# Unread products of thirteen widths in the gap behind the down projection

## The reference, cut to what matters

```python
def rmsnorm(x, g, eps=EPS):
    xf = x.astype(jnp.float32)
    y = xf * lax.rsqrt(jnp.mean(xf * xf, axis=-1, keepdims=True) + eps)
    return (y * g.astype(jnp.float32)).astype(x.dtype)

def conv_gated_ffn(h, w_gate, w_up, w_conv, w_down):
    g = causal_dwconv(h @ w_gate, w_conv)
    return (jax.nn.silu(g) * (h @ w_up)) @ w_down
...
    h = h + rmsnorm(f, g_post_ffn[layer])
...
    h = rmsnorm_2(x, norm_mix_g[l])
    proj = jnp.einsum('bsd,de->bse', h, w_in[l])
```

## Time and profile before

| what | us |
|---|---|
| median of 2 runs | 3160.98 (3160.81 to 3161.16) |
| the profiled execution: its own time | 3160.61 |
| its span, first to last instruction | 3158.8 |
| matmul engine busy | 3145.9 |
| VectorE busy | 2146.8 |
| ScalarE busy | 1823.7 |
| GpSimd busy | 457.4 |
| granted clock of the matmul engine, mean share of full speed | 0.999 |

### The profile page before, as it was taken

How to read it: one execution, slowest core, us unless ns; L and a number is a source line. 1 busy time by engine, 2 the same in 40 slices (tenths; PEclk the granted TensorE clock), 3 DMA queues, 4 the chain that set the end, 5 groups by cost and what they waited for, 6 DMA issues and landing times.

```text
span 3158.8 us, 58846 instructions
## 1 busy us (share of the span) xinstructions
PE 3145.9 (100%) x24156; PEld 3007.3 (95%) x24156; DVE 2146.8 (68%) x3503; ACT 1823.7 (58%) x2611; POOL 457.4 (14%) x317
## 2 busy tenths in 40 slices
PE   9999999999999999999999999999999999999998
PEld 9999999999999999999999999999999888888887
DVE  7987486666664477665666799855555666668886
ACT  6556554444444455555455578877777544456565
POOL 0001200000000100000000057777770000000000
PEclk9999999999999999999999999999999999999999
DMA  6444556666666656444555577787776777766554
GB/s 226 156 147 146 178 182 233 230 223 230 229 197 196 193 174 206 164 153 167 187 196 199 199 190 195 196 195 194 194 194 196 243 242 241 242 226 224 212 186 171
DMA packets 229420, 627.78 MB, mean 199 GB/s; under 512 B 59328, under 2 KB 78624, under 8 KB 229024
## 3 DMA queue, kind: packets, MB, share of 16 engines
q1 hardware_dynamic: 192144, 623.60, 59.1%
q0 software_dynamic: 36864, 0.15, 3.2%
q10 hardware_dynamic: 144, 0.26, 0.0%
HBM read 601.27 MB, written 21.10 MB: 197 GB/s over the span
## 4 chain that ended last, share of the span: by engine, by line
PE 98%; DVE 1%; ACT 1%; issue 0%; DMA 0%; POOL 0%; SPq 0%; DVEq 0%; ACTq 0%; POOLq 0%
PE ps L981 32%; PE ps L982 32%; PE ps L983 31%; DVE wl L1562 0%; PE ps L1265 0%; PE ps L1288 0%; PE ps L1285 0%; PE ps L1022 0%; PE ps L1052 0%; PE ps L1299 0%; PE ps L1289 0%; DMA raw<-in_in1k 0%; PE ps L1065 0%; PE ps L1461 0%; PE ps L1119 0%
## 5 line engine op out<-in xcount | busy, mean ns | idle before, releaser
L2402 ACT CAST wh<-raw 128x1024 fp32r<-128x1024 f32 (+3 forms) x1094 | 1137.4, 1040 | 1024.4 <-PE ps L983 1020.1
L1562 DVE TENSOR_TENSOR wl<-raw,wh 128x1024 fp32r<-128x1024 f32 (+2 forms) x863 | 1037.0, 1203 | 362.1 <-ACT wh L2402 359.5
L981 PE MATMUL ps<-xh,wh 128*128 128x256 f32 x3088 | 854.9, 277 | 0.5 <-issue 0.5
L983 PE MATMUL ps<-xh,wl 128*128 128x256 f32 x3088 | 850.0, 275 | 0.0
L982 PE MATMUL ps<-xl,wh 128*128 128x256 f32 x3088 | 849.9, 275 | 0.0
L981 PE MATMUL ps<-xw,wh 128*128 128x258 f32 (+2 forms) x2096 | 591.4, 282 | 1.8 <-issue 1.1
L983 PE MATMUL ps<-xw,wl 128*128 128x258 f32 (+2 forms) x2096 | 587.7, 280 | 0.0
L981 PEld LDWEIGHTS ps<-xh,wh 128*128 128x128 f32 x3088 | 579.7, 188 | 4.3 <-issue 1.6
L982 PEld LDWEIGHTS ps<-xl,wh 128*128 128x128 f32 x3088 | 579.8, 188 | 1.1 <-issue 1.0
L983 PEld LDWEIGHTS ps<-xh,wl 128*128 128x128 f32 x3088 | 579.6, 188 | 0.0
L2930 POOL DMA_INDIRECT table<-w_loose x256 | 397.8, 1554 | 805.3 <-DVE w_loose L2237 654.4
(11 more groups left out here) (425 smaller groups left out, 4678.0 us busy)
## 6 DMA issues: line engine op xcount, KB each, us to landing
raw<-in_peer_u SPq DMA_DIRECT2D x256, 512.0 KB, 4.7
raw<-in_peer_v SPq DMA_DIRECT2D x236, 512.0 KB, 4.2
raw<-in_w_in SPq DMA_DIRECT2D x172, 512.0 KB, 3.6
raw<-in_w_up SPq DMA_DIRECT2D x82, 512.0 KB, 4.8
raw<-in_w_gate SPq DMA_DIRECT2D x80, 512.0 KB, 4.5
raw<-in_w_down SPq DMA_DIRECT2D x80, 512.0 KB, 3.7
raw<-in_w_out SPq DMA_DIRECT2D x64, 512.0 KB, 3.7
table<-tmp SPq DMA_DIRECT2D x32, 512.0 KB, 6.3
```

Source lines behind the costliest of these rows:

```text
L981: t.matmul(o, lh, rh, start=start, stop=False)
L983: return t.matmul(o, ll, rh, start=False, stop=stop)
L1562: v.tensor_tensor(part_at(wl, i), raw[:, i % RN, 0:cols(i)], high.bitcast(F32), ALU.subtract).then_inc(lo, 1)
L2402: last = s.copy(part_at(wh, i), raw[:, i % RN, 0:cols(i)])
```

## The change

The three plain products ahead of `spread_factor` behind down go. In their place stands a new function, `unread_widths`. It waits for the first in2k chunk (`taken(I2)`), and then makes, twice over, products of 13 widths from 256 to 288 columns: for each width one group of three products for each of the seven weight tiles of that chunk. The moving side is down's rows: row n for weight tile n, read 0 columns behind its start in the first pass and 2 columns behind it in the second. A width over 256 reads on into the next row. All results go to bank 4, from its column 0, and nothing reads them. The eight plain products behind `spread_factor` stay, and so does the same gap in the middle of the first block.

```diff
+        def unread_widths():
+
+            taken(I2)
+            for m in (0, 2):
+                for w in (256, 258, 260, 262, 264, 266, 268, 270, 272, 274, 276, 280, 288):
+                    for n in range(ROWS):
+                        rh, rl = [ahl[:, PAD_A + m + FT * S * h + S * n:PAD_A + m + FT * S * h + S * n + w] for h in range(2)]
+                        three(ps[4][:, 0:w], row_at(wh, I2, n), row_at(wl, I2, n), rh, rl, True, True)
+
...
         token_squares(S, 0)
         t.wait_ge(o_sq, 32)
         token_squares(S, 5)
-        keep_busy(ps[6][:, 0:128], 3)
+        unread_widths()
         spread_factor(S, 3)
         keep_busy(ps[6][:, 0:128], 8)
```

## The result

The changed kernel takes 3229.13 us, the median of two runs (3227.86 to 3230.40), against 3160.98 before: a ratio of 1.0216, 95% interval 1.0199 to 1.0232. So it is 67 to 68 us slower; forecast were 3227.3 and a range of 3221.5 to 3232.5. The intervals take in 2%, so on which side of that line it lies stays open.

What follows compares the result with a forecast made beforehand. The matmul engine, busy 3145.9 of 3158.8 us, bounds the kernel. Block +67.3, cover -1.1, going over +0.1 give +66.3 us on the profiled 3160.61: 3226.9, and 3227.3 with the median 0.4 above; range 3221.5 to 3232.5.

Steps and rivals of the forecast that it cites:

- The cover: Wait before the factor-spreading products, 1133.56 to 1134.69 us, where the plain products stood: hides 1.13 us of the block.
- the going over: At the change from plain to split products, the next start comes after 0.20 us instead of 0.113: +0.1 us.
- The block: The 546 unread products at the seam behind down: 67.3 us, 123.2 ns a product; ends 65.0 and 70.1 us.
- the line through 119 at 258 and 125 at 272: Pitch of block products over 256 columns: straight line in ns, 0.43 ns a column, held on to 288.
- the start two columns on: Second pass of the block: taken as 0, up to 0.6 us either way on 273 products.
- the second rival: Second pass: 256-wide rows touch one more memory piece, 6.7 ns on 273 products, 1.8 us: 3229.1 us; chance 0.17.
- the signs that the prediction named: Against it: 258 to 272 at 256's pace, second pass dearer, 274 to 288 jumping, or block clock leaving 1.00.
- The weight loads: In the block: as many loads as products, as in down, and wider products leave more room; no price.
- Who waits, and what comes back: Behind the block: DVE, ACT and transfers wait, then resume at the same distances; 0 to 0.9 us won back, 0 taken.
- they lay in the wait and cost nothing: The three removed plain products ahead of the spreading: removal saves nothing itself; their 1.13 us becomes cover.
- The first rival: Block priced by columns at the clock plus at least 2.5 ns a product: 62.5 us, time 3222.5 us; chance 0.13.
- The fourth rival: The block's unread products don't run, as nothing reads them: 3161 us; chance 0.01.

Runs made afterwards that it cites:

- the 256-column places: Changed kernel with its block made 128 sets of 21 products, all 256 columns wide, at 16 row starts and 8 weight starts; 3478.62 us (one run).

## Why the prediction was right, and where it was off

**What bounds the kernel.** Right. The forecast was +66.3 us, and the seam grew by 67.4. The block's time came on top nearly whole; in all ten profiled executions with a block in the first gap, from 62 to 337 us long, block less growth of the seam is 1.23 us, to 0.005.

**The cover.** Forecast 1.13 less 0.1 for the going over, measured 1.23. From the last down product to the spreading it is the 1.13 of the forecast. The other 0.1 is behind the block: the products that spread the factor start there without a wait and take 0.61 us in the rows instead of 0.71. The 0.1 for the going over came too, and is inside the block: its first product took 0.20 us to the next start.

**The block.** Forecast 67.3 us, 123.2 ns a product; measured 68.66 us, 125.8 ns. This is the term that was mis-sized, by 1.4 us of 67; the measured block has the going over in it. The first pass was forecast at 33.65 us and took 34.05: the line through 119 at 258 and 125 at 272 was a little low at 258 (120.8) and high at 272 (123.4), and 288 came out at 132.9 for 131.9. The larger part is the second pass, 34.62 us: I had priced the start two columns on at 0, with up to 0.6 us either way, from rows whose starts differed while their weights differed too. It made 0.57 us against the first pass, and the second rival's mechanism is in it: 256 columns went from 113.7 to 121.7 ns. Its price of 6.7 ns on every product was too high, since 258, 266 and 274 columns got cheaper by about a nanosecond. So two of the signs that the prediction named as speaking against it came true: the second pass is dearer than the first, and it jumps from 126.8 ns at 274 to 133.3 at 276. That the block is off by 2% only is in part luck: the line was low at 258 and high at 272, and the start two columns on made some widths dearer and others cheaper.

**The weight loads.** "No price" was right for their number and not for their place: with the weights two columns on, 256 columns went from 113.7 to 119.8 ns in the first pass. And the 0.1136 us of the long window over down is not due to missing records: all its starts are there, most 113 or 114 ns apart and about one in twenty 117 ns or more.

**Who waits, and what comes back.** Right as far as the runs show: five runs of the changed kernel have a median 67.3 us over before, which is the growth of the seam, so as a rule nothing came back and nothing was lost behind it. Behind the seam the profiled executions have 2012.1 to 2012.5 us, before 2012.53, except four with 0.9 to 1.7 us more. Both profiled executions of the changed kernel are among the four, with that of the 256-column places and that without block and plain products, whose 0.9 us are partly the clock's. Three of them have the slow `oah` stretch, 0.7 us at the same products, two of these the wait in w_in ahead of it; the fourth is slow in the last 512 columns. Since the kernel without any block has the `oah` stretch too, the block is not needed for it. For the wait, which is in 2 of 11 executions with a block and none of 3 without, that is open.

**The removed products.** The step "they lay in the wait and cost nothing" leaves out what they bring. Left out alone, they let the clock fall, and the seam took 0.5 to 0.9 us longer; with the block in their place the clock stayed at 1.00, so that could not show.

**The line of 2%.** The seam's growth in the trace, 67.4 us, is 2.13% of 3160.98. The first rival would have needed a mean pitch under 117.6 ns, which only blocks all of 256 columns reached (113.5 and 117.0). It falls on the widths: no set of 258 columns came under 117.7 ns and none of 272 under 123.2, at any of the 128 pairs of places tried for each. The fourth rival falls too: all 546 products are in the trace.

## What to carry to other kernels

On an engine that bounds the kernel, price added products by the distance of starts in rows of the same width, and expect a jump as soon as a width leaves the one that the layout was made for: two columns more cost here as much as the next sixteen. A start moved by two or four columns can cost that jump as well, so look at the rows' start and the weights' start together, and read the pitch of the very pair from a trace before padding anything. Work that fills a wait may be worth more than nothing for what it does to the clock; take it away alone to know.

## What the runs showed of the hardware

- Some lasting pitches are 113.3, 120.0, 126.7, 133.3 ns and on to 220.0, all multiples of 6.67 ns. About three sets in ten (153 of 488) lie within 0.3 ns of one; others go through a short pattern from product to product, as 121 and 126 ns in turn at 272 columns. Why some pairs of places hold a step and others don't is not settled.
- The pattern over the rows' start moves along when the weights' start moves by 8 columns, and is another one at 4. So reading rows and reading weights may get in each other's way; that is argued from the pattern, and nothing here shows where.
- The same instructions can last through a stage at two pitches: 113.3 or 117.6 ns in the `oah` stage, 226.7 or 233.3 ns in the last 512-column stage. It makes executions of one kernel differ by 0.7 to 1.5 us with no wait to be seen. What puts a stage into one or the other was not tried.
